# The first modulation vector: products in four quarters of TensorE's columns, rows taken as they land, the context's norm moved into the mixer

## The reference, cut to what matters

```python
def ada_mod(cond, w, b):
    m = jax.nn.silu(cond) @ w + b
    return jnp.split(m[..., None, :], 6, axis=-1)

def first_block(x, c, ctx, c_ctx, ...):
    for layer in range(DEPTH):
        sh1, sc1, g1, sh2, sc2, g2 = ada_mod(c, ada_w[layer], ada_b[layer])
        ...
            csh1, csc1, ... = ada_mod(c_ctx, ada_w[layer], ada_b[layer])
            xcn = modulate(rms_norm(hc, norm_mix_g[layer]), csh1, csc1)
        xn = modulate(rms_norm(h, norm_mix_g[layer]), sh1, sc1)
        ...
            y, y_c = even_mixer(xn, xcn, mix_in_w[j], ...)   # xn @ w_in; of xcn only the k and v columns
...
def memory_cross_attention(h, mem_n, wq, wk, wv, wo, g_q, g_k):
    k = rms_norm_2((mem_n @ wk).reshape(B, M, MEM_HEADS, HEAD_DIM), g_k)
    v = (mem_n @ wv).reshape(B, M, MEM_HEADS, HEAD_DIM)
```

## Time and profile before

| | |
|---|---|
| median of 3 runs | 2358.28 us (2354.95 to 2360.48) |
| the profiled execution | 2353.65 us, of which 2351.8 us are the span that the trace shows |
| PE (matmuls) busy | 2227.9 us, 95% of the span |
| DVE, ACT, POOL busy | 46%, 32%, 4% |
| granted TensorE clock, mean | 0.972 of full speed |

### The profile page before, as it was taken

How to read it: one execution, slowest core, us unless ns; L and a number is a source line. 1 busy time by engine, 2 the same in 40 slices (tenths; PEclk the granted TensorE clock), 3 DMA queues, 4 the chain that set the end, 5 groups by cost and what they waited for, 6 DMA issues and landing times.

```text
span 2351.8 us, 25697 instructions
## 1 busy us (share of the span) xinstructions
PE 2227.9 (95%) x10940; PEld 1792.4 (76%) x10940; DVE 1081.7 (46%) x1450; ACT 757.3 (32%) x1134; POOL 87.5 (4%) x84
## 2 busy tenths in 40 slices
PE   6998999999994999999999999989999998999999
PEld 3666778888883788888888888776876676888887
DVE  3636665555537433334534333355375446443421
ACT  4314533222123322223332222223355635322211
POOL 0000000000001000000011100100000001111100
PEclk9999999999996999999999999989899998999999
DMA  7521136565620223332323322313200020333232
GB/s 262 191 82 59 64 126 192 187 194 176 202 94 29 89 91 98 98 99 94 95 91 93 104 89 92 102 56 117 72 2 1 1 90 19 107 91 107 85 99 85
DMA packets 190788, 236.64 MB, mean 101 GB/s; under 512 B 4097, under 2 KB 175393, under 8 KB 190545
## 3 DMA queue, kind: packets, MB, share of 16 engines
q1 hardware_dynamic: 189696, 230.42, 30.5%
q0 software_dynamic: 976, 4.57, 0.6%
HBM read 231.96 MB, written 2.10 MB: 100 GB/s over the span
## 4 chain that ended last, share of the span: by engine, by line
PE 88%; DVE 7%; ACT 3%; issue 1%; DMA 0%; POOL 0%; SPq 0%; DVEq 0%; ACTq 0%; POOLq 0%
PE ps L402 24%; PE ps L404 24%; PE ps L403 24%; PE ps L652 3%; PE ps L582 2%; PE ps L687 1%; PE ps L851 1%; PE ps L1001 1%; PE ps L468 1%; ACT pr L611 1%; PE ps L1982 1%; PE ps L2027 1%; DVE wl L351 1%; PE ps L381 1%; PE ps L446 1%
## 5 line engine op out<-in xcount | busy, mean ns | idle before, releaser
L402 PE MATMUL ps<-xh,wh 128*128 128x512 f32 x1800 | 713.9, 397 | 48.9 <-DVE xl L697 27.4
L403 PE MATMUL ps<-xl,wh 128*128 128x512 f32 x1800 | 706.4, 392 | 0.0
L404 PE MATMUL ps<-xh,wl 128*128 128x512 f32 x1800 | 706.4, 392 | 0.0
L351 DVE TENSOR_TENSOR wl<-raw,wh 128x2048 fp32r<-128x2048 f32 (+1 forms) x170 | 379.0, 2230 | 491.9 <-ACT wh L339 491.8
L402 PEld LDWEIGHTS ps<-xh,wh 128*128 128x128 f32 x1800 | 341.5, 190 | 128.7 <-issue 25.7
L339 ACT CAST wh<-raw 128x2048 fp32r<-128x2048 f32 (+1 forms) x170 | 314.5, 1850 | 340.1 <-PE ps L404 263.2
L404 PEld LDWEIGHTS ps<-xh,wl 128*128 128x128 f32 x1800 | 340.7, 189 | 73.0
L403 PEld LDWEIGHTS ps<-xl,wh 128*128 128x128 f32 x1800 | 341.5, 190 | 71.8 <-issue 1.2
L402 PE MATMUL ps<-hh,wh 128*128 128x512 f32 x704 | 274.1, 389 | 0.0
L404 PE MATMUL ps<-hh,wl 128*128 128x512 f32 x704 | 273.9, 389 | 0.0
L403 PE MATMUL ps<-hl,wh 128*128 128x512 f32 x704 | 273.9, 389 | 0.0
(11 more groups left out here) (329 smaller groups left out, 1799.0 us busy)
## 6 DMA issues: line engine op xcount, KB each, us to landing
raw<-in_ffn_w SPq DMA_DIRECT2D x52, 1024.0 KB, 5.4
raw<-in_ada_w SPq DMA_DIRECT2D x42, 1024.0 KB, 5.2
raw<-in_ffn_wg SPq DMA_DIRECT2D x22, 1024.0 KB, 5.4
raw<-in_ffn_wu SPq DMA_DIRECT2D x22, 1024.0 KB, 5.3
raw<-in_ffn_w SPq DMA_DIRECT2D x16, 896.0 KB, 4.9
raw<-in_ffn_wd SPq DMA_DIRECT2D x16, 896.0 KB, 4.8
raw<-in_w_in SPq DMA_DIRECT2D x10, 1024.0 KB, 5.2
raw<-in_ffn_wd SPq DMA_DIRECT2D x8, 1024.0 KB, 5.1
```

Source lines behind the costliest of these rows:

```text
L351: e.tensor_tensor(wl[s][:, 0:n], r[:, 0:n], wh[s][:, 0:n].bitcast(F32), ALU.subtract).then_inc(*WLO.up(i))
L402: e.matmul(dst, ah, bh, start=start, stop=False)
L403: e.matmul(dst, ah, bl, start=False, stop=False)
L404: return e.matmul(dst, al, bh, start=False, stop=stop)
```

## The change

The eight pieces are no longer multiplied in a row. Each of the four products of a piece goes to 32 columns of the array of its own, by the 32 partitions of PSUM that it writes; the stationary operand is `scp` with 32 columns, of which 2 are not zero. The four quarters of bank 4 (scale: bank 3) hold partial results, which eight small fp32 products with a matrix of ones and zeros (`pick`) add and turn. All pieces land in buffers of their own: the seventh in a new `fb6`, the eighth in the memory's buffer `mmT` once that has been used, and the context comes into `fb5` after piece 5 has been multiplied. The units of kind `first` are gone, so `in0` is unit 2. The context's sums stand ahead of tile c = 4 on PE, its spread ahead of c = 5.

```diff
-        fb = [sb(f"fb{n}", [P, 2, 1024], F32, part) for n in range(6)]
-        ctT = sb("ctT", [P, NC, LC], F32, part)
+        fb = [sb(f"fb{n}", [P, 2, 1024], F32, part) for n in range(7)]
+        ctT = fb[5][:, :, :].rearrange("p a b -> p (a b)").rearrange("p (c t) -> p c t", c=NC)
...
             sp_unit(e, 0)
+            first_rows(0)
+            first_rows(1)
             sp_unit(e, 1)
...
+            for n in range(2, 6):
                 first_rows(n)
             sp_unit(e, 2)
+            first_rows(6)
+            e.wait_ge(*VX["mem", 7])
+            first_rows(7)
+            e.wait_ge(*MM["first", 5])
+            e.dma_start(ctT[:, :, :], A["ctxT"].rearrange("(c p) t -> p c t", p=P)).then_inc(*LAND["ctx"].landed("ctx"))
             sp_unit(e, 3)
...
         def act_prologue(e):
+            act_squares(e, "x", xT, T, LAND["x"]["x"], None, None)
             for c in range(2):
...
+            act_root(e, "x", 3, 1, T, D)
...
             act_weights(e, of["in", 0])
+            e.wait_ge(*MM["first", 7])
+            e.copy(tmp[3][:, :], pb[3]).then_inc(*AE.up("first rows"))
...
             act_weights(e, of["in", 1])
+            act_squares(e, "ctx", ctT, LC, LAND["ctx"]["ctx"], VX["x", 7], MM["first turned"])
...
+        def dve_context(e):
+            dve_inverse(e, "ctx", 0, 1, LC)
+            e.wait_ge(*LAND["masks"]["masks"])
+            e.tensor_copy(bcs[:, :], bst[:, :]).then_inc(*VF.up("masks"))
             e.wait_ge(*VF["factors", "ctx"])
+            dve_norm(e, "ctx", ctT, LC, lambda c: cf[:, 8 + c:9 + c], lambda c: adac[:, c:c + 1], mh, ml, 6)
...
         def pe_first(e, n):
             for kk in range(2):
                 for h in range(2):
-                    m = e.matmul(pb[4][0:8, :], scp[:, 2 * j + h, 2 * k + kk, :], w[:, kk, h * 512:(h + 1) * 512],
-                                 start=n == 0 and kk == 0 and h == 0, stop=n == 5 and kk == 1 and h == 1)
+                    q = 32 * (2 * kk + h)
+                    m = e.matmul(pb[4 - j][q:q + 32, :], scp[:, 2 * k + kk, :], fb[n][:, kk, h * 512:(h + 1) * 512],
+                                 start=k == 0, stop=k == 3)
...
         def pe_mix_in(e):
+                    if c == 4:
+                        pe_context_sums(e)
+                    if c == 5:
+                        pe_context_spread(e)
...
         def act_mix_in(e):
                 if n:
                     act_ahead(e, u)
+                if n == 2:
+                    act_context(e)
                 for cc in range(2):
                     c = 2 * n + cc
+                    if c == 5:
+                        act_norm(e, "ctx", mh, LC, lambda c: adac[:, c:c + 1])
...
         def dve_mix_in(e):
             for n in range(1, 4):
                 dve_ahead(e, of["in", n])
+                if n == 2:
+                    dve_context(e)
```

More of the change, by code:

```diff
@@ L36 @@
 NVEC = _at
-CST = {"ident": 0, "ones": 128, "bd": 256, "eps": 384, "one": 385, "freq": 386, "valid": 387, "zero": 388, "half": 389}
-NCST = 390
+CST = {"ident": 0, "ones": 128, "bd": 256, "eps": 384, "one": 385, "freq": 386, "valid": 387, "zero": 388, "half": 389, "pick": 390}
+NCST = 394
 BCS = {"ident": 0, "diag": 128, "prev": 256, "sbm": 384, "cmp": 512}
@@ L99, in weight_units @@
     w_cols("mv", A["mem_wv_2"][0], 0, 256)
-    for k in range(2, 4):
-        ada("first", 0, 1, k)
     ada0 = [(0, j, k) for j in range(2, 6) for k in range(4)]
@@ L735, in sp_unit @@
                     e.wait_ge(*WLO[i - 2])
-                elif units[i - 2].kind == "ada":
+                else:
                     e.wait_ge(*VA[i - 2])
-                else:
-                    e.wait_ge(*MM["first", i - 2 + 4])
             dst = raw[i % 2][:, 0:u.kc * u.cols].rearrange("p (k n) -> p k n", k=u.kc)
@@ L775, in act_prologue @@
             both = vec[:, 0:16].rearrange("p (z k) -> p k z", z=2)
-            for q in range(4):
-                e.activation(scp[:, q, :, 2 * q:2 * q + 2], both, ACT.Silu).then_inc(*AF.up(("silu", q)))
+            e.activation(scp[:, :, 0:2], both, ACT.Silu).then_inc(*AF.up("silu"))
             e.activation(sc[:, :, :], both, ACT.Silu).then_inc(*AF.up("silu c"))
@@ L873, in pe_prologue, with pe_context_sums, pe_context_spread @@
             pe_head_spread(e, ("km", 1), 2, LC, 1)
[L874 to L882 removed]
+            pe_first(e, 6)
+            pe_first(e, 7)
+            pick = cst[:, CST["pick"]:CST["pick"] + 4]
+            for j, (src, ready) in enumerate(((ssum, VF["first rows"]), (tmp[3], AE["first rows"]))):
+                e.wait_ge(*ready)
+                for c in range(4):
+                    o = (j * 4 + c) * 4
+                    m = e.matmul(pb[4][:, o:o + 4], src[:, c * P:(c + 1) * P], pick, start=True, stop=True)
+            m.then_inc(*MM.up("first turned"))
+        def pe_context_sums(e):
             e.wait_ge(*VF["square", "ctx", 7])
             pe_sums(e, "ctx", ssum, 1, LC)
+        def pe_context_spread(e):
             e.wait_ge(*VF["inverse", "ctx"])
[L886 to L892 removed]
+            pe_spread(e, "ctx", 0, 1, LC, 6)
         def pe_mix_in(e):
@@ L2395, in constants @@
     cst[:, CST["valid"]] = r >= 31
+    cst[:, CST["pick"]:CST["pick"] + 4] = (r[:, None] % 64) == (np.array([0, 1, 32, 33])[None])
     masks = np.zeros((P, NBCS), f)
```

91 lines of the change are left out of this document (35 added, 56 removed).

## The result

The kernel after takes **2332.18 us** (median of 4 runs, 2326.58 to 2337.72); the kernel before took 2356.61 in the same rounds (4 runs, 2354.53 to 2360.48). The ratio is 0.9894 (from 0.9866 to 0.9922 with 95% confidence); the medians lie 24.4 us apart. Forecast was 2337 (2329 to 2347), with 0.93 on faster. The profiled execution after took 2333.21 us, its span is 2331.4 us.

What follows compares the result with a forecast made beforehand. The prologue was taken as bound by PE streaming 512 columns repeatedly for 8 rows of result. T 25.7 us sooner less 4.3 given back in the mixer is 21.4, so 2358.28 became 2337 us, range 2329 to 2347.

Steps and rivals of the forecast that it cites:

- T: End of the prologue: the moment DVE starts the norm of x, 76.16 us in the first profile before.
- A piece of 1.05 us: Prologue on PE: a piece's four products on column quarters take 1.05 us, against 3.5 us one after another.
- two-halves row: Trace of L687 before: two 256-column products on 64 array columns each, four records in 0.65 us, one taking 0.379.
- pairs only: Rival, prologue pieces: four quarters do no better than two halves, 1.75 us a piece, 2340.5 us; 14% with loads between products.
- in a row: Rival, prologue pieces: products do not overlap, 3.5 us a piece, T at 66.5, total 2353 us; chance 6%.
- T at 50.5, 25.7 sooner: Prologue: the new path through pieces, values, keys, copy and picks puts DVE's norm of x at 50.5 us, 25.7 sooner.
- 50 to 51: Sign in the new profile: DVE's first norm op of x stands at 50 to 51 us.
- The mixer gives back 4.3: Mixer: the moved context costs 0.5 sums, 2.4 stall before its spread, 0.7 spread and 0.7 clock, 4.3 us.
- No stall: Rival, mixer: in2 and in3 land sooner or the clock holds, 3.1 us come back, 2334 us; chance 12%.
- Late transfers: Rival, prologue: pieces wait for transfers, piece 7 at 50 instead of 45 moves T by 4, 2341 us; chance 7%.
- The clock: Rival, slower: PE's idle moments lower its clock; all eight mixer tiles at half clock would give 2375 us; chance 3%.
- The sum: Whole kernel: 25.7 less 4.3 is 21.4 us sooner, from a median of 2358.28 to 2337 us.

Runs made afterwards that it cites:

- before_again: The kernel before, unchanged, profiled a second time: 2359.61 us (one run).
- halves: The changed kernel with two column halves of 64 columns per round instead of four quarters: 2336.88 us (one run).
- serial: The changed kernel with its new order and landings, but each piece's products one after another on 8 columns as before: 2348.04 us, ratio 0.9959.
- context_only: The kernel before with only the context's sums, inverse and norm moved into the mixer: 2359.60 us, ratio 1.0003.
- again: The changed kernel once more, for a second profile and more timed rounds: 2332.69 us, ratio 0.9890.
- inverse_early: The changed kernel with the context's root on ACT and inverse on DVE ahead of the two halves of in3: 2329.39 us, ratio 0.9878.
- quarters_only: The kernel before with column quarters and the eight pick products alone; order, landings and context as before: 2347.58 us, ratio 0.9942.
- inverse_early_2: The kernel of inverse_early once more, for comparison with one_bank: 2331.72 us, ratio 0.9892.
- one_bank: inverse_early with all rows in one bank, four pick products of 8 columns and no copy on ACT: 2329.57 us, ratio 0.9885.

## Why the prediction was right

**The time, from like profiles.** before_again took 2359.61 us and after 2333.21, 26.4 less: T is 27.7 sooner, the rotation 1.6 closer to T before than after, and from there to the end 0.3 apart. The first profile before makes 20.4 of it (28.1 less 2.6 less 5.1), because by chance its clock stayed full in the late steps; the comparison by medians is 24.4.

**A piece of 1.05 us.** Measured 1.07, and 1.92 for two. The two-halves row carried over to four quarters; halves and serial give 1.94 and 3.60 on the same data, so the rivals *pairs only* and *in a row* describe kernels that exist, and this is not one of them. All four quarters use all 128 rows, and their four products take 1.07 us where one alone takes 0.87 (two records of 0.436). The Trainium skill ("TensorE: Matmul & The Clock Gate", Part 3) states that a weight load overlaps with matmuls in flight only where the row group differs. This trace does not agree: by that rule the piece would have taken 1.75 us. A piece of serial over one of after is 3.60 / 1.07 = 3.4 times. The prediction had estimated 3.1 from the 2.38 times that the Trainium skill gives in the same part for three column tiles.

**T at 50.5, 25.7 sooner.** Measured 48.09, 28.1 sooner; 1.7 of that is the late first landing of the first profile before, which is luck, and 26.4 are left (27.5 against before_again). With 1.7 us off for the first landing, the forecast's path was: tile 0 of the values done at 30.1 (measured 30.2), x's squares 32.6 (32.5), x's spread done 37.8 (37.4), pieces 4 and 5 done 40.5 (40.3), keys scaled 42.9 (42.8), the copy done 45.9 (45.6), picks done 48.0 (47.6), T 48.8 (48.09). No step is off by more than 0.7. The forecast of 2.1 us for the `pick` products held as well (2.02). That pieces 0 and 1 cost nothing was right though they took 1.93 us each: the memory's spread was not pushed (it comes 8.0 us behind the start of the memory's squares, as in before_again, which has no piece ahead of it). The sign "50 to 51" was missed all the same: with a first landing as late as in the first profile before, T would be 49.8.

**The mixer gives back 4.3.** This was the mis-sized term: sums 0.5, spread 0.7, pause 2.4, clock 0.7. By the column "rest", sums and spread are 36.3 less 35.0 to 35.5, 0.8 to 1.3 us: right. The pause was 1.33 (1.33 to 1.93 in the five profiles that have it), below the 2 to 3 us that the prediction named as a sign of being right. (By its own terms PE wanted the spread at T + 31.9, 25.9 + 0.5 + 5.5, and not 31.8.) Its mechanism was as forecast, down to T + 24.0 for the issue of in3 (forecast 24.1); the landing took 5.1 us in place of the 5.8 of the earlier trace rows, which is most of the 1.1 that were too many, and PE came for the spread at T + 32.1, 0.3 later. The clock's 0.7 was zero: it stayed at 1.00 behind the pause. The row from which this term was taken did not show what a pause does, since in after the clock fell before the pause of 2.89 us and not in it. The other half-clock stretch, behind T, was there before and after and differs between executions of one kernel by as much as 1.5 us.

**The rivals.** *No stall*: the stall was there, but halfway to it. *Late transfers*: piece 7 was waited for by 0.16 to 0.84 us, never by 4. *The clock*: the mixer did not get slower by it. In all five profiles with a pause in the mixer the 4 us from the spread on had 1.00, and from the rotation to the end after takes 2243.8 us and before_again 2244.1. In the profile after, the window of 133.5 to 141.5 us has 0.79, which took 1.7 us; before_again, context_only and serial have the same 0.79 there, again, inverse_early and halves have 1.00.

**The sum.** By these parts it is 26.4 at T less 2.2 in the mixer (rest 0.83, pause 1.33), 24.2 us (24.8 by the same parts of before_again), where 21.4 was forecast and the medians say 24.4. The forecast of 2337 is 5 us high: 3 us are these terms, 1.7 the median of before, 2356.61 in the rounds that were compared and 2358.28 in those of the forecast. The interval of the ratio is 13 us wide, so that comparison alone would not tell 21.4 from 24.4; that of again, 22.6 to 29.5 us, leaves 21.4 out, as the parts do. The lower end of the range was worked wrongly: the case with no stall, 2334, less 3 is 2331 and not 2329. The measured 2332.18 lies inside by either. **What stays open** is what makes the clock fall, and why in one execution and not in the next.

## What to carry to other kernels

Here a product with 2 useful columns in the stationary operand took as long as its 512 streamed columns did, and four of them on the four column quarters of the array took little more than one (1.07 us against 0.87). That pays in full only if what stands behind it in the other engines' order is moved as well: here the quarters alone gave 12 to 13 us at T, the order alone 11 to 12, both together 26 to 27, since each alone left another wait. When a chain becomes shorter, look for tiny instructions that stand in order behind large ones which wait for a transfer (0.16 us of inverse behind 2.3 us of low half), and compare two profiles of the same kernel before you put a microsecond down to a change.

## What the runs showed of the hardware

- Eight fp32 records of 512 columns: 3.60 us in a row on 8 columns of the array (serial), 1.94 on halves, 1.07 on quarters (after). The first piece of each, in the first 20 us, took 6.39, 3.68 and 1.93, the 6.39 only in part at the lower rate.
- In all eleven profiles the clock was at half for most of the first 4 us of the mixer (0.50 to 0.65 on average), which took 1.4 to 2.9 us, and PE had paused for 2.9 us ahead of the mixer. When it fell differs. In after, again and inverse_early it fell before that pause, with PE busy on the `pick` products and no wait of more than 1.14 us since the first piece. In quarters_only it was at half already in those products. In both profiles of before, inverse_early_2, halves and one_bank it fell within the pause (0.61 to 0.90 on average over it), and in context_only and serial only when the mixer ran (1.00 through the pause). Pauses of 1.3 to 1.9 us in the mixer were followed by 1.00 in all five profiles that have one.
- One execution of a kernel may have full clock where the next has 0.91 over 20 us; two such places make some 3 of the 6 us between the spans of the two profiles of the kernel before.
